# Two stacked transformer blocks on one core: left-over tokens' values in float32 on quarters of the array, blocks 1 and 2 made in halves, and another order in the last norm

## What is computed

```python
h = jnp.concatenate([meta, x], axis=1)                 # 272 tokens
xn = rms_norm(h, norm_gains[layer, 0])
proj = xn @ w_in[layer]
q_a, k_a, v_a, f_a, q_b, k_b, v_b, g_a, g_b = jnp.split(proj, SPLIT_POINTS, axis=-1)
...
gate_p = jax.nn.sigmoid(rms_norm_2(x, g_ple[i]) @ w_ple_gate[i])
x = x + gate_p * (p[i] @ w_ple[i])
...
return rms_norm_2(x, g_final)
```

## Time and profile before

| | |
|---|---|
| median of 3 runs | 910.97 us (910.88 to 911.46) |
| profiled execution | 911.43 us |
| its span, first to last instruction | 910.2 us |
| TensorE busy | 901.4 us |
| VectorE busy | 681.8 us |
| ScalarE busy | 479.0 us |
| GpSimd busy | 59.4 us |
| mean granted clock of TensorE | 0.998 |

### The profile page before, as it was taken

One profiled execution on the slowest core, in us unless ns is written; L12 is line 12 of the kernel. 1 busy time (PEld: TensorE's weight loads), 2 busy tenths in 40 slices (PEclk: granted clock), 3 DMA queues, 4 the chain that ended last, 5 costly groups with the idle time before them and its releaser, 6 DMA issues.

```text
span 910.2 us, 17845 instructions
## 1 busy us (share of the span) xinstructions
PE 901.4 (99%) x7210; PEld 870.5 (96%) x7210; DVE 681.8 (75%) x1206; ACT 479.0 (53%) x844; POOL 59.4 (7%) x123
## 2 busy tenths in 40 slices
PE   9999999999999999999999999999999999999997
PEld 7899989999999999998999989999999999999997
DVE  8775676779888878889799877786768666666676
ACT  5366354555655445466465744554335544444456
POOL 6023000120000000000000000000102000000001
PEclk9999999999999999999999999999999999999999
DMA  8553443546556656555644363655646666666651
GB/s 320 179 159 117 139 133 119 178 139 180 158 178 203 183 169 203 181 174 179 194 149 124 116 205 119 185 185 173 187 152 185 206 188 186 185 186 185 186 156 53
DMA packets 42689, 154.72 MB, mean 170 GB/s; under 512 B 4720, under 2 KB 5232, under 8 KB 42480
## 3 DMA queue, kind: packets, MB, share of 16 engines
q1 hardware_dynamic: 42608, 153.59, 54.6%
HBM read 152.52 MB, written 1.05 MB: 169 GB/s over the span
## 4 chain that ended last, share of the span: by engine, by line
PE 97%; DVE 1%; DMA 1%; ACT 0%; SPq 0%; issue 0%
PE bank L272 96%; DMA raw<-in_wts 1%; DVE wl L1326 0%; PE bank L825 0%; PE bank L452 0%; DVE va L1955 0%; PE bank L663 0%; PE bank L664 0%; PE bank L456 0%; PE bank L455 0%; PE bank L665 0%; PE bank L454 0%; PE bank L453 0%; DVE qk L1664 0%; SPq L2026 0%
## 5 line engine op out<-in xcount | busy, mean ns | idle before, releaser
L1326 DVE TENSOR_TENSOR wl<-raw,wh 128x1024 fp32r<-128x1024 f32 x284 | 351.4, 1246 | 94.7 <-ACT wh L868 92.8
L868 ACT ACTIVATE wh<-raw 128x1024 fp32r<-128x1024 f32 x248 | 259.5, 1054 | 159.2 <-PE bank L272 148.9
L272 PE MATMUL bank<-a2h,wh 128*128 128x256 f32 x896 | 253.8, 284 | 0.1
L272 PE MATMUL bank<-a2h,wl 128*128 128x256 f32 x896 | 250.5, 280 | 0.0
L272 PE MATMUL bank<-a2l,wh 128*128 128x256 f32 x896 | 248.5, 280 | 0.0
L272 PE MATMUL bank<-a1h,wh 128*128 128x258 f32 (+1 forms) x800 | 226.1, 284 | 0.7 <-issue 0.6
L272 PE MATMUL bank<-a1h,wl 128*128 128x258 f32 (+1 forms) x800 | 223.7, 281 | 0.0
L272 PE MATMUL bank<-a1l,wh 128*128 128x258 f32 (+1 forms) x800 | 220.2, 282 | 0.0
L272 PEld LDWEIGHTS bank<-a2h,wh 128*128 128x128 f32 x896 | 168.8, 188 | 3.2 <-issue 2.9
L272 PEld LDWEIGHTS bank<-a2h,wl 128*128 128x128 f32 x896 | 168.6, 188 | 0.0
L272 PEld LDWEIGHTS bank<-a2l,wh 128*128 128x128 f32 x896 | 167.6, 188 | 0.3
(11 more groups left out here) (245 smaller groups left out, 1007.9 us busy)
## 6 DMA issues: line engine op xcount, KB each, us to landing
raw<-in_wts SPq DMA_DIRECT2D x284, 512.0 KB, 3.8
csb<-in_cst SPq DMA_DIRECT2D x1, 1428.0 KB, 10.0
out<-va SPq DMA_DIRECT2D x2, 512.0 KB, 3.0
xc<-in_xT SPq DMA_DIRECT2D x1, 544.0 KB, 5.5
raw<-in_wts SPq DMA_DIRECT2D x2, 256.0 KB, 3.3
xc<-in_xT SPq DMA_DIRECT2D x1, 276.0 KB, 3.0
xc<-in_xT SPq DMA_DIRECT2D x1, 272.0 KB, 4.3
va<-in_pT SPq DMA_DIRECT2D x1, 256.0 KB, 3.9
```

The costliest lines, as they stand in the source:

```text
L272: return e.matmul(o, lhsT, rhs, start=start, stop=stop, skip_group_check=True)
L868: e.activation(wh[:, i % NHL, :], raw[:, i % NRAW, :], ACT.Copy).then_inc(s_hi, 1)
L1326: e.tensor_tensor(lo, src, hi.bitcast(F32), ALU.subtract).then_inc(s_lo, 1)
```

## The change

1. Left-over tokens. The matmuls on `a1h` are gone. GpSimd now multiplies the 16 columns by the norm's gain in float32 into `tokf` (a view of `va[:, 6]`), as soon as the tokens have landed. After every second block (q = 1 and 3), TensorE makes four float32 matmuls, one for each of four k-tiles, with `raw` itself as moving operand. The one for k-tile j of the four uses columns 32j to 32j+31 of the array and writes rows 32j to 32j+31 of the bank. The four parts are added at the output: a copy and three additions on 16 x 512.
2. Loads 4 to 11 wait in addition for TensorE's count of finished blocks, since `raw` is read by it.
3. Blocks 1 and 2 are made in halves of 512 columns, block 1 by VectorE and block 2's high halves by ScalarE.
4. The outputs of v_a: copy and the two large multiplies by ScalarE in tile 0, the three additions and the small multiply by VectorE after tile 1. Waits on `s_va` are renumbered.
5. Last norm: GpSimd adds four squares. Turns 0 to 4 come before the sums, turn 5 before the last sum and turns 6 and 7 behind it.

```diff
@@ values
-                    if i0 + q:
+                    if i0 + q > 2:
                         e.wait_ge(s_lo, i0 + q + 1)
...
-                        if meta is not None:
-                            e.wait_ge(s_meta, 4 * k + 2 + (2 if m0 == 0 else 0))
-                            mm(bank[meta][:, :], a1h[:, k, m0:m0 + 128], mh, k == 0, False)
-                            t = mm(bank[meta][:, :], a1h[:, k, m0:m0 + 128], ml, False, k == KT - 1)
+                        if meta is not None and kk and q % 2:
+
+                            e.wait_ge(s_meta, 2 * k + (1 if m0 else 2))
+                            for j in range(4):
+                                t = mm(bank[meta][32 * j:32 * j + 32, :], tokf[:, k - 3 + j, m0:m0 + 32],
+                                       raw[:, (i0 + q - 1 + j // 2) % NRAW, j % 2 * 512:j % 2 * 512 + 512], q == 1, q == 3)
@@ tensor_engine, last norm
-            for n in range(3, 6):
-                turn_out(n)
+            turn_out(3)
+            turn_out(4)
             e.wait_ge(s_rs, 7)
-            e.wait_ge(s_sqp, Q_FIN + 3)
+            e.wait_ge(s_sqp, Q_FIN + 4)
             token_sum(qk[:, 0, 0:S], True, False)
-            for m in (4, 5, 6, 7):
-                if m == 6:
-                    turn_out(6)
+            for m in (5, 6, 7):
+                if m == 7:
+                    turn_out(5)
...
-            turn_out(7)
+            for n in range(6, 8):
+                turn_out(n)
@@ scalar_engine
+                if k == 5:
+
+                    e.wait_ge(s_raw[2], 16)
+                    e.activation(wh[:, 2, 0:512], raw[:, 2, 0:512], ACT.Copy).then_inc(s_h2, 1)
+                    e.activation(wh[:, 2, 512:1024], raw[:, 2, 512:1024], ACT.Copy).then_inc(s_hi, 1)
+                    made["n"] = 3
...
                 if t == 0:
+                    e.wait_ge(s_blk, B_VA + 4)
+                    e.wait_ge(s_rtc0, 6)
+                    e.wait_ge(s_vp, 4)
+                    e.activation(va[0:NM, 3, :], bank[3][0:NM, :], ACT.Copy).then_inc(s_vp, 1)
+                    for c in range(2):
+                        e.activation(va[:, 4 + c, :], bank[4 + c][:, :], ACT.Identity,
+                                     scale=r_tok0[:, 2 + c:3 + c]).then_inc(s_va, 1)
                     forget()
@@ vector_engine
+                if k == 2:
+                    e.wait_ge(s_raw[1], 16)
+                    half_hi(1, 0, s_h1)
+                    half_lo(1, 0, s_h1, 1, s_l1)
+                    half_hi(1, 512, s_hid)
+                    half_lo(1, 512, s_hid, 1, s_lo)
+                elif k == 4:
+                    half_lo(2, 0, s_h2, 1, s_l2)
+                elif k == 5:
+                    half_lo(2, 512, s_hi, 2, s_lo)
...
+            def meta_out(n, d, o, r_meta, copied):
+
+                if not copied:
+                    e.wait_ge(s_pad, 3)
+                    e.tensor_copy(d, o[0:NM, :]).then_inc(s_vp, 1)
+                for j in range(1, 4):
+                    e.wait_ge(s_vp, n + j)
+                    e.tensor_tensor(d, o[32 * j:32 * j + NM, :], d, ALU.add).then_inc(s_vp, 1)
+                e.wait_ge(s_vp, n + 4)
                 e.tensor_scalar(d, d, r_meta[0:NM, :], None, ALU.mult).then_inc(s_vm, 1)
...
-            values_out(B_VB, 0, lambda c: va[:, (2, 0, 1)[c], :], 0, (1, 2), r_tok0[:, 0:2], r_tok0[:, 4:5])
+            e.wait_ge(s_blk, B_VB + 4)
+            meta_out(0, va[0:NM, 2, :], bank[0], r_tok0[:, 4:5], False)
+            for c in range(2):
+                e.tensor_scalar(va[:, c, :], bank[1 + c][:, :], r_tok0[:, c:c + 1], None, ALU.mult).then_inc(s_va, 1)
             for q in range(4):
                 lo_to(B_VA + q + 4)
-            values_out(B_VA, 4, lambda c: va[:, 3 + c, :], 3, (4, 5), r_tok0[:, 2:4], r_tok0[:, 5:6])
...
+                if t == 1:
+                    meta_out(4, va[0:NM, 3, :], bank[3], r_tok0[:, 5:6], True)
@@ gpsimd_engine
-            e.wait_ge(s_init, 2)
-            e.wait_ge(s_pad, 1)
+            e.wait_ge(s_pad, 4)
             for k in range(KT):
-                e.wait_ge(s_xhi, k + 1)
-                e.tensor_copy(a1h[:, k, 128:128 + NM], xnh[:, k, S:L]).then_inc(s_meta, 1)
...
+                e.wait_ge(s_x[X_PART[k]], 16)
+                for n, t0 in enumerate((S, 0)):
+                    e.tensor_scalar(tokf[:, k, 32 - 32 * n:32 - 32 * n + NM], hT[:, k, t0:t0 + NM], g0[:, k:k + 1], None,
+                                    ALU.mult).then_inc(s_meta, 1)
...
-            square_add(Q_FIN, 0, lambda m: 1 + m % 4, 3, S, 52)
+            square_add(Q_FIN, 0, lambda m: 1 + m % 4, 4, S, 52)
@@ sync_engine
             def load(i):
                 if i >= NRAW:
                     e.wait_ge(s_lo, i - NRAW + 1)
+                if NRAW <= i < B_F + NRAW:
+
+                    e.wait_ge(s_blk, (i - NRAW) // 2 * 2 + 2)
                 e.dma_start(raw[:, i % NRAW, :], wts[i]).then_inc(s_raw[i % NRAW], 16)
```

More of the change, by code:

```diff
@@ L179, in program @@
         s_x = [sem("s_x0"), sem("s_x1"), sem("s_x2")]
-        s_rawa, s_h0, s_l0 = sem("s_rawa"), sem("s_h0"), sem("s_l0")
+        s_rawa, s_h0, s_h1, s_h2 = sem("s_rawa"), sem("s_h0"), sem("s_h1"), sem("s_h2")
+        s_l0, s_l1, s_l2 = sem("s_l0"), sem("s_l1"), sem("s_l2")
         s_col, s_cst, s_lam, s_p, s_out = sem("s_col"), sem("s_cst"), sem("s_lam"), sem("s_p"), sem("s_out")
@@ L192, in program @@
         s_rtc0 = sem("s_rtc0")
+        s_vp = sem("s_vp")
         s_va, s_evA, s_evD = sem("s_va"), sem("s_evA"), sem("s_evD")
@@ L232, in ev2 @@
             return (s_evA if c == "A" else s_evD), EV1.count(c) + EV2[:t + 1].count(c)
+        tokf = va[:, 6, :].rearrange("p (k c) -> p k c", k=KT)
         FD = lambda m: bank[4 + m // 2][:, (m % 2) * S:(m % 2) * S + S]
@@ L325, in values @@
                         k = 2 * q + kk
-                        if i0 + q == 0:
-                            e.wait_ge(s_lo if kk else s_l0, 1)
+                        if i0 + q <= 2:
+                            if kk:
+                                e.wait_ge(s_lo, i0 + q + 1)
+                            else:
+                                e.wait_ge((s_l0, s_l1, s_l2)[i0 + q], 1)
                         mh, ml = wh[:, s, kk * 512:kk * 512 + 512], wl[:, s, kk * 512:kk * 512 + 512]
@@ L362, in sb_scores @@
                 if pair == 0:
-                    e.wait_ge(s_va, 8)
+                    e.wait_ge(s_va, 4)
                     e.wait_ge(s_vm, 2)
@@ L504, in tensor_engine @@
                 if t == 0:
+                    e.wait_ge(s_vp, 4)
+                elif t == 1:
+                    e.wait_ge(s_va, 1)
+                elif t == 2:
                     e.wait_ge(s_va, 2)
[L506 to L509, removed]
                 elif t == 3:
@@ L645, in diff_scores @@
                 if h == 0:
-                    e.wait_ge(s_va, 10)
+                    e.wait_ge(s_va, 6)
                 else:
@@ L672, in diff_av @@
                 if h < 2:
-                    e.wait_ge(s_va, 12)
+                    e.wait_ge(s_va, 8)
                 else:
@@ L1349, in input_lo, with half_hi, half_lo @@
                 weighed_lo(N_IN, k, xnl[:, k, :], xnh[:, k, :], hT[:, k, :], 0, g0)
-            def first_lo(c, made_hi, done):
-                e.wait_ge(made_hi, 1)
-                e.tensor_tensor(wl[:, 0, c:c + 512], raw[:, 0, c:c + 512], wh[:, 0, c:c + 512].bitcast(F32),
+            def half_hi(i, c, done):
+                e.tensor_copy(wh[:, i, c:c + 512], raw[:, i, c:c + 512]).then_inc(done, 1)
+            def half_lo(i, c, made_hi, n, done):
+                e.wait_ge(made_hi, n)
+                e.tensor_tensor(wl[:, i, c:c + 512], raw[:, i, c:c + 512], wh[:, i, c:c + 512].bitcast(F32),
                                 ALU.subtract).then_inc(done, 1)
             e.wait_ge(s_rawa, 16)
-            e.tensor_copy(wh[:, 0, 0:512], raw[:, 0, 0:512]).then_inc(s_h0, 1)
-            first_lo(0, s_h0, s_l0)
+            half_hi(0, 0, s_h0)
+            half_lo(0, 0, s_h0, 1, s_l0)
             input_lo(0)
             input_lo(1)
-            first_lo(512, s_hi, s_lo)
-            made["n"] = 1
+            half_lo(0, 512, s_hi, 1, s_lo)
+            made["n"] = 3
             for k in range(2, KT):
-                if k == 3:
-                    lo_to(2)
                 input_lo(k)
+                if k == 2:
[8 more added lines that the diff above has]
+                    half_lo(2, 512, s_hi, 2, s_lo)
                 if k % 2:
@@ L1958, in gpsimd_engine @@
         def gpsimd_engine(e):
-            e.memset(a1h[:, :, 128:256].bitcast(F32), 0.0).then_inc(s_pad, 1)
+            e.memset(tokf, 0.0).then_inc(s_pad, 1)
             e.memset(kb[:, :, L:384], 0.0).then_inc(s_pad, 1)
```

18 lines of the change are left out of this document (2 added, 16 removed).

## The result

| | before | changed |
|---|---|---|
| median | 911.12 us (910.88 to 911.46, 4 runs) | 919.67 us (919.00 to 921.56, 4 runs) |
| ratio | | 1.0097, 95% interval 1.0084 to 1.0109 |
| profiled execution | 911.43 us | 920.19 us |
| its span | 910.2 us | 918.9 us |
| mean granted clock of TensorE | 0.998 | 0.994 |

A forecast was written before the change was run, and what follows sets the result against it. TensorE, busy 901.4 of 910.2 us, was taken as the bound. Opening +6.5 and last norm -0.5 give +6.0 on the profiled 911.43, so 917.4; the median, 0.46 lower, is 917.0 us, range 914.5 to 921.5.

The forecast's parts named there:

- Matmuls: Value projections: four float32 groups at 1.25 us each cost 5.0 us, replace 7.5 us; TensorE's own work falls by 2.5.
- rival of quarters one after another: Float32 groups in the projections: the four quarters run in turn, 3.9 us a group, 923.6 us in all; chance 0.04.
- estimate of 1.5 us: Float32 groups: 4 x 0.88 / 3.07 + 0.37 us each by the skill's row-tile figure, making the forecast 0.5 us later.
- To the second projection: Opening: TensorE waits for VectorE's tree of squares before the input sum; second projection starts at 22.3 us, not earlier than 22.16.
- First hold: Opening: load 6 waits for the first projection's end, making block 7's low half late; stall 3.6 us, first ordinary tile +2.55.
- Behind the first stall: From block 7's start to the first ordinary tile: block 7 and its group take 4.05 us, tile starts at 39.6.
- a rival at 0.08: TensorE's clock falls at both opening stalls, each costing about 2.0 us more: 921.0 us; chance 0.08.
- Second hold: Before sb_scores: loads 10 and 11 wait for the group behind block 7; stall 3.9 us, +6.5 in all.
- Last norm: End of kernel: four records of sums leave TensorE, but VectorE's last square limits the gain to -0.5 us.
- VectorE is slowed a little under it, and had 0.4 us spare: Final norm: GpSimd's fourth square, 0.77 us under the last gate tile, only slightly slows VectorE, which has 0.4 us spare.
- slow landing: Opening: load 6 or load 10 lands late, +2.4 us each, 919.4 or 921.8 us for both; chance 0.10.
- The other rivals: Whole kernel: TensorE's lighter work gives 908.0 us, 0.06; late load landings 919.4 or 921.8, 0.10; no effect 911, 0.02.
- TensorE's own saving decides: Whole kernel: TensorE's lighter work, -2.5 and -0.5 us, gives 908.0 us if low half 7 is early; chance 0.06.

## Why the prediction held, step by step

Forecast 917.0 (914.5 to 921.5), measured 919.67: the sign and the range held, the size was short by 2.7 us. The sum was made against the profiled execution: forecast +6.0, there +8.8.

- **Matmuls: right.** A group costs 1.19 us (forecast 1.25): 1.00 from 12.58 to the next start, and the matmuls on either side of it take 0.33 and 0.34 us from start to start instead of 0.233. The rival of quarters one after another is out by experiment. The estimate of 1.5 us from the factor 3.07 of the Trainium skill (TensorE: Matmul & The Clock Gate, Measured speedup vs the span model) was too high. That factor is for row tiles; on these column tiles in float32 four quarters take 1.00 us where four in turn take 3.56, a factor of 3.56 with the change of tiling included.
- **To the second projection: right.** The sum waited until 19.19 (forecast 19.1), the projection started at 22.23 (22.3), and the first projection's saving was lost there.
- **First hold: right.** Load 6 issued 22.41 (22.5), landed 25.95 (26.3), low half 6 until about 28.2 (28.6), outputs until 34.1 (34.3), low half 7 until 35.2 (35.55), stall 3.4 (3.6).
- **Behind the first stall: the step that failed.** F0 was forecast 4.05 us behind block 7's start and came 5.28 behind it (35.34 to 40.62). The missing 1.23 us is the clock at half from 34.82 to 38.23. The forecast had this as a rival at 0.08, with 2.0 us a stall, and took full speed as likelier since before shows no wait over 1 us. It is what happened, at 1.2 and 1.5 us instead of 2.0.
- **Second hold: mechanism right, shifted by the clock.** Load 10 was issued at 40.80 (39.85) and landed at 44.37 (43.65). sb_scores waited 3.5 us (3.9). Its lag of 7.40 less 1.23 is 6.2, forecast 6.5. Behind it the clock costs the second part: the next tile lags 8.91, so 1.5 more. At the last gate matmul the lag is 8.74, 1.34 more than at sb_scores; that difference is less sharp, since between these two places kernels that differ in nothing there took 852.8 to 854.0 us.
- **Last norm: wrong, -0.5 forecast, 0.0 measured.** The step that failed is "VectorE is slowed a little under it, and had 0.4 us spare". The multiply is not slowed a little but ends 0.29 us after GpSimd's addition, however much of it lies beside: it takes 0.55 us more, and that delay doesn't stay on VectorE: ScalarE's order turns it into a later sigmoid of the last tile. In the kernel before there was no square of tile 6 late enough to stand in front. The run with the sigmoid first brings 0.37 of the 0.5.

The sum over the steps: 6.2 of waiting less the saving, 1.2 and 1.5 of clock: 8.9 at 58.95, of which the last gate matmul shows 8.7, and 0.0 at the end. The error of 2.8 against the profiled execution is the clock (2.6 as far as the last gate matmul shows it) and the last norm (0.5), less 0.3 that the stalls came shorter. 919.67 lies inside the range because the range was made wide enough for most of a slow landing or of the clock; the sum alone gave less. The other rivals did not occur: loads 6 and 10 took 3.5 and 3.6 us to land, and TensorE's own saving decides only once nothing is held.

## What to carry to other kernels

When a second engine comes to read a transfer buffer, follow the buffer: the cost of the float32 matmuls was not on TensorE (it gained) but on the load that had to wait for it, and then on every instruction of an in-order engine that stood behind the late block. An engine that others wait for and that is itself idle just before is the sign; the repair is another buffer, or work that needs no transfer moved into the hole. And a stall of several microseconds on TensorE is to be priced with the clock that it costs: 1.2 and 1.5 us here, and 3.2 and 3.8 us behind the shorter waits of 2.4 to 2.5 us, where the clock stayed at half for twice as long.

## What the runs showed of the hardware

- The granted clock behind waits. By the idle times in the brackets, it fell to 0.50 (1.2 GHz) at TensorE's waits of 3.24 and 3.33 us in the change, for 3.41 us each time, and at waits of 2.46 and 2.38 us in two other kernels, for 6.83 us. It stayed at 1.00 (2.4 GHz) behind waits of 1.19, 1.29 and 1.37 us in three kernels, and with the stalls filled by matmuls on a constant. In the change the half speed began at 34.82, before the stall had ended, and at 55.30, after it had.
- VectorE beside GpSimd. The multiply of two float32 tiles of 128 x 256 takes 0.42 us alone. Started during an addition of GpSimd it ends 0.29 us after the addition does, so it takes 0.63 us when it starts late in one (907.88, in the addition that ends at 908.22) and 0.97 when it starts 0.1 us into one (908.89, in the addition that ends at 909.57). The instruction at 907.54, which reads one of its inputs from a bank, takes 0.42 us beside the same addition. The Trainium skill (GPSIMD Engine Reference, Specifications) says that GpSimd's path to SBUF is shared with VectorE and contends with VectorE's instructions on two SBUF inputs; the trace agrees, with 0.55 us for one addition of 0.78.
